# Identity products at stage edges, an earlier rounding in odd_out, and counting shared between VectorE and ScalarE in the key selection of a two-layer decoder step

## Time and profile before

| engine | busy us | share of the span | instructions |
|---|---|---|---|
| TensorE (PE) | 3246.2 | 88% | 17291 |
| its weight loads (PEld) | 2584.5 | 70% | 17291 |
| VectorE (DVE) | 1803.8 | 49% | 3171 |
| ScalarE (ACT) | 1403.3 | 38% | 2389 |
| GpSimd (POOL) | 152.6 | 4% | 168 |

### The profile page before, as it was taken

One profiled execution on the slowest core, in us unless ns is written; L12 is line 12 of the kernel. 1 busy time (PEld: TensorE's weight loads), 2 busy tenths in 40 slices (PEclk: granted clock), 3 DMA queues, 4 the chain that ended last, 5 costly groups with the idle time before them and its releaser, 6 DMA issues. The chain is left out here.

```text
span 3669.5 us, 44268 instructions
## 1 busy us (share of the span) xinstructions
PE 3246.2 (88%) x17291; PEld 2584.5 (70%) x17291; DVE 1803.8 (49%) x3171; ACT 1403.3 (38%) x2389; POOL 152.6 (4%) x168
## 2 busy tenths in 40 slices
PE   8879994876978799999998998996888799999996
PEld 6724642444776699899886677674786699899885
DVE  5677998632335544444444431056335444444543
ACT  6452212632344433433444441153334333433443
POOL 0020110033000000000000000012000000000000
PEclk9989996997989899999999897997999899999998
DMA  3122122056031333343352210012020433333452
GB/s 103 25 66 81 42 74 78 1 181 221 24 99 57 121 130 123 115 134 119 127 161 81 64 35 24 23 25 80 23 104 30 144 123 130 115 128 125 127 161 105
DMA packets 226195, 341.90 MB, mean 93 GB/s; under 512 B 34375, under 2 KB 163119, under 8 KB 225988
## 3 DMA queue, kind: packets, MB, share of 16 engines
q1 hardware_dynamic: 214212, 297.13, 25.1%
q0 software_dynamic: 11776, 41.95, 3.5%
HBM read 328.56 MB, written 10.19 MB: 92 GB/s over the span
## 5 line engine op out<-in xcount | busy, mean ns | idle before, releaser
L638 DVE TENSOR_TENSOR s_mlp_w2l<-s_mlp_w2b,s_mlp_w2h 128x1024 fp32r<-128x1024 f32 x192 | 235.1, 1226 | 585.1 <-ACT s_mlp_w2h L524 585.1
L172 PE MATMUL ps<-s_mlp_xl,s_mlp_w1h 128*128 128x384 f32 (+1 forms) x1536 | 499.3, 325 | 9.0 <-DVE s_mlp_xl L656 9.0
L174 PE MATMUL ps<-s_mlp_xh,s_mlp_w1h 128*128 128x384 f32 (+1 forms) x1536 | 495.9, 323 | 0.0
L173 PE MATMUL ps<-s_mlp_xh,s_mlp_w1l 128*128 128x384 f32 (+1 forms) x1536 | 495.4, 323 | 0.0
L524 ACT CAST s_mlp_w2h<-s_mlp_w2b 128x1024 fp32r<-128x1024 f32 x192 | 201.5, 1050 | 588.8 <-PE ps L174 588.7
L172 PE MATMUL ps<-s_mlp_w2l,s_mlp_hh 128*128 128x512 f32 x1024 | 406.0, 396 | 20.5 <-DVE s_mlp_hl L675 16.2
L174 PE MATMUL ps<-s_mlp_w2h,s_mlp_hh 128*128 128x512 f32 x1024 | 403.1, 394 | 0.0
L173 PE MATMUL ps<-s_mlp_w2h,s_mlp_hl 128*128 128x512 f32 x1024 | 403.0, 394 | 0.0
L172 PEld LDWEIGHTS ps<-s_mlp_xl,s_mlp_w1h 128*128 128x128 f32 x1536 | 289.8, 189 | 41.1 <-issue 34.9
L173 PEld LDWEIGHTS ps<-s_mlp_xh,s_mlp_w1l 128*128 128x128 f32 x1536 | 289.8, 189 | 6.2
L174 PEld LDWEIGHTS ps<-s_mlp_xh,s_mlp_w1h 128*128 128x128 f32 x1536 | 289.6, 189 | 0.0
(11 more groups left out here) (559 smaller groups left out, 5589.0 us busy)
## 6 DMA issues: line engine op xcount, KB each, us to landing
s_mlp_w1b<-w_ff SPq DMA_DIRECT2D x96, 1024.0 KB, 6.2
s_mlp_w2b<-w_ff SPq DMA_DIRECT2D x96, 1024.0 KB, 8.4
x_kb<-cache_mem_k SPq DMA_DIRECT2D x16, 512.0 KB, 7.1
x_vb<-cache_mem_v SPq DMA_DIRECT2D x2, 4096.0 KB, 20.6
s_orows_raw<-w_in_odd SPq DMA_DIRECT2D x32, 256.0 KB, 3.0
s_convsel_w<-w_in_even SPq DMA_DIRECT2D x12, 512.0 KB, 3.9
x<-x_prompt SPq DMA_DIRECT2D x8, 512.0 KB, 5.6
ev_mixT<-w_in_even SPq DMA_DIRECT2D x16, 256.0 KB, 4.1
```

Of the source, the lines that this page charges most:

```text
L172: nc.tensor.matmul(out, ah, bl, start=first, stop=False, skip_group_check=True)
L173: nc.tensor.matmul(out, al, bh, start=False, stop=False, skip_group_check=True)
L174: return nc.tensor.matmul(out, ah, bh, start=False, stop=last, skip_group_check=True)
L638: nc.vector.tensor_tensor(w2l[:, s % RING], w2b[:, c % 3, s % FC, :], w2h.bitcast(F32)[:, s % RING], ALU.subtract).then_inc(low2, 1)
```

## The change

It has three parts.

1. `keep_warm(nc, G, bank, n)` is new: n plain float32 products of the identity with four copies of itself, 512 columns each, into a PSUM bank that is free at that point; nothing reads them. They stand in TensorE's stream: 3 before the first sample piece and 4 at the end of each `stage_out`; 9 before the six turns and 4 after them in each MLP; 14 at the end of mlp0 alone; 7 at the start of qkg; 3 at the start and 4 at the end of mlstm. That is 82.
2. In odd_out, the rounding and the split of tile 1 now stand ahead of `tail_sample` and of VectorE's wait for the gain, as they do in the other three output stages.
3. In convsel the three widest tiles (1024, 896, 768 columns) are no longer counted by VectorE. It only writes the comparison's marks, ahead of the sample count; ScalarE adds each tile's marks up by a copy with an accumulator, and VectorE waits for the three sums at the round's end. The half products are spread evenly over 32 rounds (2, 2, 2, 3 of them), the memory's transposes stand at rounds 8, 16, 24, 31, its 32 weight tiles behind all counting, `gate_in` in rounds 5, 13, 21, 29. ScalarE's stream is written by rounds. The final selection does the sample tile first.

The diff, cut to its core:

```diff
+def keep_warm(nc, G, bank, n):
+    for _ in range(n):
+        nc.tensor.matmul(G.ps[:, bank, :].rearrange("p (a t) -> p a t", a=4), G.ident[:], bc(G.ident[:].unsqueeze(1), [P, 4, P]),
+                         start=True, stop=True)
...
 # stage_out, TensorE
+            keep_warm(nc, G, 2, 3)
             sample(0)
...
+            pe.wait_ge(added, NT - RING + 2)
+            keep_warm(nc, G, 2 * (NT % RING), 4)
 # stage_out, ScalarE (VectorE's rest_of_tile likewise)
-            if not rows:
-                round_tile(1)
+            round_tile(1)
             tail_sample()
             for t in range(NT):
-                if rows and t + 1 < NT:
+                if rows and 1 <= t < NT - 1:
                     round_tile(t + 1)
 # stage_mlp, TensorE
+            keep_warm(nc, G, 7, 9)
             for e in range(6):
                 turn(e, e)
+            keep_warm(nc, G, 7, 4)
             up(0)
...
+            if name == "mlp0":
+                keep_warm(nc, G, bank(), 14)
 # stage_conv_select
-        TURN_AT = (8, 14, 20, 24)
-        FIRST = 25
+        TURN_AT = (8, 16, 24, 31)
+        def done(x):
+            return 9 * (x + 1) // 4
 # TensorE
-            for x in range(ROUNDS):
-                for i, hk in halves[3 * x:3 * x + 3]:
+            for x in range(ROUNDS - 2):
+                for i, hk in halves[done(x - 1):done(x)]:
                     half_product(i, hk)
                 if x in TURN_AT:
                     turn_mem(TURN_AT.index(x))
-                if x >= FIRST:
-                    for q in range(4 * (x - FIRST), min(4 * (x - FIRST) + 4, 4 * KD)):
-                        mem_product(q)
...
                 add_segments(x)
+            for x in (ROUNDS - 2, ROUNDS - 1):
+                add_segments(x)
...
+            for q in range(4 * KD):
+                mem_product(q)
 # ScalarE
+            def sum_marks(x):
+                for m, s in enumerate(shared):
+                    act.wait_ge(marked, len(shared) * x + m + 1)
+                    v = marks[:, mark_at[s]:mark_at[s] + SEL[s][1]]
+                    nc.scalar.activation(v, v, ACT.Copy, accum_out=cnt[:, s:s + 1]).then_inc(summed, 1)
...
+            for x in range(ROUNDS - 2):
+                sum_marks(x)
...
+                for i in range(done(x - 1) // 2, done(x) // 2):
+                    if i % 9 // 3 != 1:
+                        evict(i)
+                    if i % 9 == 8:
+                        if i == 35:
+                            gain_mem(3)
+                        taps(i // 9)
 # VectorE, count()
+                for s in shared:
+                    wd = SEL[s][1]
+                    nc.vector.tensor_scalar(marks[:, mark_at[s]:mark_at[s] + wd], scores[:, OFF[SEL[s][0]]:OFF[SEL[s][0]] + wd],
+                                            thr[:, s:s + 1], None, ALU.is_ge).then_inc(marked, 1)
                 nc.vector.tensor_scalar(junk[:], C.sc, thr[:, n_sel:n_sel + 1], None, ALU.is_ge, ALU.add,
                                         accum_out=cseg[:, 0:1]).then_inc(counted, 1)
-                for j, (t, wd) in enumerate(SEL):
+                for j in (2, 1, 0):
...
                 sum_segments(cnt[:, n_sel:n_sel + 1])
+                dve.wait_ge(summed, len(shared) * (x + 1))
...
-                if x % 6 == 4 and x < 24:
-                    gate_in(x // 6)
+                if x % 8 == 5:
+                    gate_in(x // 8)
...
-            for j, (t, wd) in enumerate(SEL + [(NT, W)]):
+            for j in (n_sel,) + tuple(range(n_sel)):
 # qk_gates, TensorE
+            keep_warm(nc, G, 7, 7)
             pe.wait_ge(side_in, 64)
 # mlstm, TensorE
+            keep_warm(nc, G, 7, 3)
             pe.wait_ge(made, 2)
...
+            pe.wait_ge(inter_kept, N)
+            keep_warm(nc, G, 3, 4)
```

More of the change, by code:

```diff
@@ L358, in _ @@
                 nc.vector.tensor_tensor(wl[:, k], raw[:, k % 4], wh.bitcast(F32)[:, k], ALU.subtract).then_inc(w_low, 1)
-            if not rows:
-                rest_of_tile(1)
+            rest_of_tile(1)
             dve.wait_ge(gain_in, 16)
@@ L1235, in stage_conv_select @@
         junk = S.sb("junk", [P, W])
-        junk2 = S.sb("junk2", [P, SEQ])
+        junk2 = S.sb("junk2", [P, SEL[2][1]])
+        shared = (5, 4, 3)
+        marks = S.sb("marks", [P, sum(SEL[s][1] for s in shared)])
+        mark_at = {s: sum(SEL[u][1] for u in shared if u > s) for s in shared}
         us, acc, z = B.qiT[:, 0, :], B.qiT[:, 1:3, :], B.qiT[:, 3, :]
@@ L1271, in stage_conv_select @@
                                "tail_made", "tail_turned", "tail_kept", "stored"))
+        marked, summed = S.sem("marked"), S.sem("summed")
         counted, total, pool_link, zs_made, tapped, gated = (
@@ L1377, in _ @@
                 add_segments(x)
[L1378 to L1382, removed]
+            for x in (ROUNDS - 2, ROUNDS - 1):
+                add_segments(x)
+            pe.wait_ge(m_gained, 16)
+            pe.wait_ge(tail_made, 4)
+            for n in range(4):
+                ins = nc.tensor.transpose(G.ps[0:18, 7, n * P:(n + 1) * P], tail[:, n, :], G.ident[:])
+            ins.then_inc(tail_turned, 1)
+            for q in range(4 * KD):
+                mem_product(q)
         @block.scalar
@@ L1406, in _, with evict, taps @@
             act.wait_ge(side_kept, 2)
[L1407 to L1427, removed]
+            def sum_marks(x):
[3 more added lines that the diff above has]
+                    nc.scalar.activation(v, v, ACT.Copy, accum_out=cnt[:, s:s + 1]).then_inc(summed, 1)
+            def evict(i):
+                n, j, c = i // 9, i % 9 // 3, i % 3
+                act.wait_ge(product, i + 1)
+                src = G.ps[:, i % 6, 0:CW]
+                if j == 0:
+                    if n >= 1:
+                        act.wait_ge(z_made, 3 * n)
+                    nc.scalar.copy(us[:, c * CW:(c + 1) * CW], src).then_inc(u_kept, 1)
+                else:
+                    nc.scalar.copy(A.mixT[:, n, c * CW:(c + 1) * CW], src).then_inc(gb_kept, 1)
+            def taps(n):
                 act.wait_ge(z_made, 3 * n + 3)
```

24 lines of the change are left out of this document (17 added, 7 removed).

## The result

The changed kernel takes 3651.2 us (median of 13 runs, 3644.17 to 3689.93). Timed again beside it, the kernel before took 3693.92 (13 runs, 3671.28 to 3702.71); its three runs shown ahead of the prediction were among its shortest. The ratio is 0.9923, 95% interval 0.9898 to 0.9947: 28 us faster, 20 to 38, of the 3688 that the runs before average. The groups of short executions (near 3672 and 3651) lie 21 us apart, the shortest of each 27. Forecast were 45.5 us and 3626, range 3604 to 3650. The direction was right; the measured time lies 1.2 us outside the range, and 25 above the forecast.

A forecast was written before the change was run, and what follows sets the result against it. TensorE was taken as the bound, winnable where it idles or runs at half clock. Key selection 21, odd_out 8.5 and identity products 6 + 5.5 + 2 + 2 + 0.5 sum to 45.5 us: from 3671.36 to 3626, range 3604 to 3650.

The forecast's parts named there:

- the sum of the rounds: Key selection: 31 rounds of 5.81 us plus 8.7 and 2.7 end at 519.8, 43.6 us earlier; 21 kept.
- ScalarE's sums: Key selection: three sums take some 3.1 us a round, 1.18 for the widest, and end about 1 us before VectorE needs them.
- the 2.7 that I allowed: Key selection: ScalarE's runs of taps delay a round by 0.9 us, three times.
- the 8.7: Key selection: extras of the rounds expected to stay, from 11.6 us before, less some 2.9 for TensorE.
- The lower bound of 16: Key selection: 16 us kept instead of 21 if the three plain comparisons take longer, saving 1.16 us a round, not 1.40.
- The new wait: odd_out: TensorE waits 4 us at tile 2, its rounding behind tile 0's tail; gain 8.5, or 6.5 if the clock falls.
- Identity products: Stage edges: 82 added products gain 6 in the MLPs, 5.5 mlstm, 2 qkg, 2 xo0 and xo1, 0.5 mlp0's end.
- Rival (a): qkg: the gates keep the full clock that identity products give them, 12 us more, 3614; chance 0.13.
- mlstm's 5.5: mlstm: three products ahead bring rounds of 8.81 and 5.70 us to 4.86; gain 5.5, 0 if the clock falls.
- (b): Key selection: ScalarE's sums late by the whole 1.40 saved every round, 3669, or 3647 at half; chance 0.10.
- (e): odd_out: part two fails and tile 1 still waits, 3634; chance 0.04.
- (c): Stage edges: identity products are lost, the clock having fallen again when work comes, 3642; chance 0.09.
- (d): Key selection: pauses in each round drop TensorE to half clock in the counting, slower, 3776; chance 0.04.

The follow-up runs named there:

- e3_nine: Changed kernel with nine single convolution products in each of 32 rounds instead of 2, 2, 2, 3 halves of four; 3637.43 us, ratio 0.985.
- e5_no_pool: Changed kernel with GpSimd's five tap additions and products of each of the four groups left out; 3631.8 us (one run).
- e1_no_warm: Changed kernel without any of its 82 identity products; 3659.58 us, ratio to the kernel before 0.9944.
- e6_tile2: Changed kernel with tile 2 of odd_out also rounded and split one step earlier, ahead of tile 0's tail; 3644.27 us, ratio 0.9874.
- e2: Kernel before with the 82 identity products alone, key selection and odd_out as before; 3661.54 us, ratio 0.9947.
- e8_hold: Changed kernel with each mlstm unit doing its wide product three times instead of once; 3655.93 us, ratio 0.993.
- e13_before_hold: Kernel before with each mlstm unit doing its wide product three times instead of once; 3685.47 us, ratio 1.0028.
- e12_hold_one: Changed kernel with nine convolution products a round, odd_out's tile 2 early and one more wide product in each mlstm unit; 3633.27 us, ratio 0.9866.

## Why the prediction was wrong

**Key selection, the step that failed: the sum of the rounds.** The round itself (5.79 for 5.81), ScalarE's sums and the tail of memory products (56.18 for 56.9) were right; between the rounds' end and attend, 2.8 us less passed than I gave. But the rounds' extras were 17 us more, in two terms that I put at nothing: TensorE's lateness, and GpSimd.

TensorE's 2.25 halves of a round I took as a mean, 5.5 under 5.81, with pauses of 0.2 us, and let the clock stay up. Eight rounds have three halves, 7.35 us. That alone makes none late: in rounds 7 and 23, at full clock, TensorE hands over in time; in round 7 its products begin 2.4 us ahead of VectorE's round (362.67 against 365.08), in round 27, behind the slow round 26, only 1.0 ahead. The other six were late by 0.9 to 2.2 us, 8.9 together, and in each the clock was down in that round or the one before. In the seven profiles with this spread of the halves, all 42 such rounds with half clock near them were late, by 0.7 to 2.1 us, and of the 14 without it none, but for round 31 twice (0.45; it also holds four transposes). Before each fall TensorE had paused: 1.9 us behind VectorE's gate products, 4.3 in a round that GpSimd stretched, 2.2 at the start. Not each such pause brought one: behind the gate products of rounds 5 and 21 the clock stayed up. With nine single products a round (e3_nine) the lateness went, though two of its rounds still ran at half clock in part.

GpSimd I priced at nothing, since its queue isn't changed. In rounds 8, 16, 24 its additions stretch the bit step from 0.17 to 1.85, in 9, 17, 25 the comparisons from 1.88 to 3.92: 3 x 3.7 = 11.2 us, which e5_no_pool shows. ScalarE's lateness behind the taps was 3 x 1.07 = 3.2, near the 2.7 that I allowed, and the gate products took 5.2 of the 8.7. 8.9 + 11.2 + 3.2, less the 6.2 that I had for such things, is the 17 us. As the memory products stand behind the rounds, nothing hid them. The lower bound of 16 was also worked out wrongly: 0.24 us more in each of 31 rounds leaves 13.5 of the 21.

That slowing could have been read in the kernel before. Of its 11.6 us of extras I gave 2.9 to TensorE; but in rounds 1 to 31 VectorE waits for TensorE nowhere, and 6.0 us are narrow steps of VectorE in rounds 6, 12, 17 and 23 that end as an instruction of GpSimd ends. Round 17, 2.24 us in place of 0.17, with GpSimd beside it:

```profile
457.33 2.24 DVE L1213 TENSOR_SCALAR s_convsel_inc<-s_convsel_cnt 128x7 int32<-128x7 f32 x1
457.20 2.35 POOL L1461 TENSOR_TENSOR ev_qiT<-ev_qiT 128x1023 f32<-128x1023 f32 x1 [6.19 <-ACT s_convsel_tap L1434]
```

The row of 748 ns has no GpSimd beside it; the counts that it replaces run through GpSimd's work unharmed. The Trainium skill has the rule in "SBUF — State Buffer", section "SBUF: two separate sides": VectorE and GpSimd share one pair of ports, held exclusively by whichever starts, and VectorE asks for it in its fast mode with two ports or with two SBUF inputs. The runs agree: the step of round 17 ends at 459.57, GpSimd's addition at 459.55; the plain comparison was slowed, 1.88 to 3.92 and 5.85, and no accumulating count was (of 192 before, the longest took 1.28). That the plain comparison runs in the fast mode and the count doesn't, no run shows.

**Between attend and mlp0** 4.8 of the 6.9 us were gone again in the profiled execution: sattend waited for its gathers, and some of its transposes then ran at half clock. In the thirteen other profiles the way from attend to even_out, which no variant touches, scatters by 7 us, so I take it for chance; nothing here shows its cause.

**odd_out.** Tile 2 starts 42.2 us after the stage's first turn, 50.0 before: 7.7 for 8.5. The new wait was forecast at 4, it is 6.2, and the clock fell in it. Over the stage 4.8 us were left, under the 6.5 that I gave for that case. This profile lies at the low end: in the seven others with this odd_out the wait is 2.6 to 5.9 us and the stage 5.4 to 6.7 shorter than before, in e1_no_warm, without identity products, 3.9 and 6.2. The cause was the one named, the tail and finish of tile 0 (e6_tile2).

**Identity products.** Forecast 16, measured 8 to 10 (e1, e2). From the first turn to the first down product, mlp0 is 3.1 us and mlp1 2.6 shorter in the changed kernel, as forecast, but only 1.0 to 1.5 in about half of the other profiles. The gates gained nothing here, and 3 us in six others; I had 2. Rival (a) is refuted by these six: behind the seven products the gates begin at full clock (16 records in 1.8 us), and from the third 16 on they take 3.4. mlstm's 5.5 was the term with the wrong model: I gave it a lower bound of nothing, and the stage scatters by 29 us. Of the eight profiles with the three products and no others in the stage, four have full clock throughout (71.1 to 71.2 us), four lie 14 to 29 us above; three without them took 78.4, 78.4 and 98.2. With the products the clock is up at the first unit in all eight, without them it is down in all three; in four of the eight it falls some 2 us later and stays down for 31 to 65 us.

**The base.** I subtracted from 3671.36, one of the short executions; on its 13 runs that kernel averages 3688. The gain in ratio, 28 us, holds 60% of the 45.5; the absolute time misses by 25. The base doesn't explain that miss, as short against short the gain is 21 to 27: some 14 us lie in the key selection, 2 to 4 in odd_out and 6 to 8 in the identity products.

**Rivals.** (b) and (e) did not come: ScalarE was not late by the whole saving, tile 1 no longer waits. (c) came for the part of the 16 us that the products didn't earn, and (d) in small: the clock fell in the rounds, for 27 us and not for a third of them. Open remains what decides in an execution whether mlstm loses the clock; e8_hold and e13_before_hold show that it makes the spread, not what starts it.

## What to carry to other kernels

When work is spread over rounds that hand over in each, compare the longest share with the round, not the mean, and at half clock too if the engine pauses ahead of it. When an instruction changes its form on VectorE, look at what GpSimd does at that time, even if GpSimd's code is untouched. And before a forecast of one per cent, ask for the spread of the base: one stretch that lies at either clock by chance can be larger than the change.

## What the runs showed of the hardware that was not expected

- A stage whose TensorE was busy 59.60 of 60 us lay at granted clock 0.50 for all of it, and the same code lay at 1.00 in other executions (unit time 8.8 against 4.85 us). Two more wide products in each unit kept it at 1.00 from start to end when it began there (e8_hold); one more did not, in the profile of e12_hold_one.
- A gate record of 16 columns takes 1.85 / 16 = 0.116 us at full clock and 3.43 / 16 = 0.214 at half. By the Trainium skill ("TensorE: Matmul & The Clock Gate", "LDWEIGHTS (loading the stationary operand)") a load of 128 columns takes P / 1.2 = 107 ns, with no clock named; at full clock the row lies near that, at half clock twice as high, so here it is no floor that holds at both.
- A copy with accumulation on ScalarE costs 1.06 us for 1024 columns, VectorE's accumulating count 1.20: for this type an adding pass costs the two about the same. The move isn't even for that, since VectorE still compares: it saves VectorE 1.4 us a round and costs ScalarE 2.9.
- A step of VectorE on 7 columns took 1.85 and 2.24 us in place of 0.17 beside GpSimd's additions, until the addition ended; an accumulating count of 1024 columns at such times took its usual 1.28.
